# Ninety-six-slot expert units in a two-block network kernel, with the overflow blocks looped in threes

## The chip, the core and the metric

The kernel runs on one core of a Trainium2 chip. The metric is device time in microseconds (us), lower is better. A median of three runs is given; one further execution was taken by the hardware profiler and gives every row shown here.

## The reference, cut to what matters

The network has 512 tokens of width 1024. The first block ends in a mixture of experts, and that part is what the change touches:

```
logits = xt @ router_w + router_b                 # 512 tokens x 32 experts
top_val, top_idx = lax.top_k(logits, 4)           # every token goes to 4 experts
gate = softmax(top_val)
gu   = xblk @ w_gu[e] + b_gu[e]                   # 1024 -> 2048: gate half g, up half up
act  = (min(up, 7, -7 clipped) + 1) * (g * sigmoid(1.702 * g)),   g = min(g, 7)
y    = act @ w_down[e] + b_down[e]                # 1024 -> 1024
out[token] += y * gate                            # over the 4 experts of a token
```

So there are 2048 token places over 32 experts, 64 on average. For the inputs as they are drawn, the router of the reference gives expert 0 21 tokens, and the other 31 experts, the fullest first: 173, 125, 102, 101, 94, 94, 93, 89, 86, 85, 80, 80, 76, 72, 66, 64, 61, 60 and so on down to 5. All arithmetic is in 32-bit floats. The second block (attention, a state-space scan, a convolutional feed-forward part) follows and isn't touched.

## The kernel before, in words

**Units.** The experts are worked off in 33 units, in a fixed order that the core knows before it has seen the tokens (`expert_units`, L45 to L53). Expert 0 comes first; the others are ranked by their number of tokens on the core, and a unit belongs to a rank. A large unit has 128 slots (expert 0 and the ranks 0 to 14), a small one has 64 (the ranks 15 to 30, and one more for the tokens 128 to 191 of rank 0). Large and small units alternate: even unit numbers are large, odd ones small, the last (32) is small. A token that finds no slot goes to an extra block of 128 slots after the units; `dve_extra_lists` (L1646) makes the list of them, 16 long, from the capacities in `RANK_CAPS` (L58).

**A unit on TensorE (PE).** Weights come as panels of 1024 x 512 (2 MB each): two for the gate half, two for the up half, two for down. The tokens' features are the stationary operand and the weight panel is the moving one. In a large unit (`pe_expert_in`, L1773; `pe_expert_out`, L1805) each panel takes 8 matmuls of 128 slots x 512 columns, one after the other. In a small unit the 64 slots are put in twice: the lower 64 columns of the array work on the first panel while the upper 64 work on the second, so that one pass of 8 steps covers both panels, and the result has slots of the first half of the columns in partitions 0 to 63 and of the second half in 64 to 127. Here a "beat" is one 32-bit pass of 512 moving columns; a matmul in 32-bit floats is two records in the profile and takes two beats.

**The order on PE** (`pe_moe`, L1858): gate(u), down(u-1), up(u), then the next u. Smaller work is put in between the steps (`between`): the transposes of the activations of u-1 in gate(u); in up(u) the matmuls that make the slot list of u+2 (`pe_slots`, L1488, 4 matmuls against the 0/1 matrix `sel`), the transposes of the gathered tokens of u+1, and the shares of u-1. A **share** (`pe_share`, L1840) sends the result of an expert back to the tokens: per 128 features a one-pass matmul of a high and a low part against `tokens_r`, four visits of two feature tiles each. A share of a small unit uses the array in two row halves that work at once, and waits until both of its PSUM banks are free (L1850).

**The other engines.** VectorE (DVE) clips the gate and up results, multiplies, and adds each share to `hidden` (L1946), which frees the bank for the next share. ScalarE (ACT) copies transposes and scales results. GpSimd (POOL) gathers the tokens of unit u by an indirect DMA and lays out the expert columns for the bias. SyncE (SP) loads the weight panels in order into six slots; each load waits until PE has given the slot back (`Panels.load`, L172).

**The extra blocks.** `extra_blocks` (L2005) is a loop of 16 turns on each of PE, ACT, DVE and SP. Each turn reads the block's number from memory and branches over the body when it is zero. DVE moves the common counter `turn` on for a skipped block, and ACT and SP wait for 16 blocks' worth of it before the next stage (L2107, L3350, L2204); PE has to leave its own loop.

Of the kernel before, what the change touches and what calls it, by code (L numbers as in the profile page):

```python
# [14 lines left out]
P = 128  # L15
# [28 lines left out]

def expert_units():  # L45
# [12 lines left out]
RANK_CAPS = [(NE, S), (NE - 1, HALF - S), (15, S - HALF), (1, HALF)]  # L58
# [168 lines left out]
def constants():  # L227
# [16 lines left out]
    parts["block_start"] = np.broadcast_to(S * np.arange(-1, XBLOCKS)[None, :], (P, XBLOCKS + 1))  # L244
# [30 lines left out]
def build(nc, a, table, where, out):  # L275

    ctx = ExitStack()
    with ctx:
# [25 lines left out]
        with ExitStack() as over:  # L304
# [4 lines left out]
            tokens_r = over.enter_context(nc.sbuf_tensor("tokens_r", [P, T], F32R))  # L309
            perm_r = over.enter_context(nc.sbuf_tensor("expert_of_rank", [P, 2, NE], F32R))  # L310
            both_r = over.enter_context(nc.sbuf_tensor("expert_of_unit", [P, 3, S], F32R))
        IOTA_AT = 8192 + 3 * D + T + 2 * NE + 3 * S
# [987 lines left out]
        router_w = part(IOTA_AT + T, DT, NE)  # L1300
        r_at = [IOTA_AT + T + DT * NE]

# [6 lines left out]
        logits, cur, hot, cand, chosen, expo, im64, posm, posr, perm = (r_part(TT, NE) for _ in range(10))  # L1309
# [5 lines left out]
        cmp_t = r_part(16, NE)  # L1315
        bgu = r_part(NE, 16)
        slot_vals = r_part(N_UNITS, 2)
        slot_tok = r_part(N_UNITS).bitcast(I32)
        unit_expert = r_part(N_UNITS)[0:1, :].bitcast(I32)
        extra_e = sb("extra_expert", [1, 16], I32)  # L1320
        extra_b = sb("extra_block", [1, 16], I32)
# [33 lines left out]
        def chunks(u):  # L1355
            return UNITS[u][2] // HALF
# [8 lines left out]
        def small_no(u):  # L1365
            return sum(chunks(v) == 1 for v in range(u))
# [121 lines left out]
        def pe_slots(pe, mm, banks, u):  # L1488
# [3 lines left out]
            for t in range(TT):  # L1492
                vals = gate_0[:, t, :] if u == 0 else gate_r[:, t, r:NE + 1:NE - r]
                ins = mm(bank[:, 0:2], sel[:, u % 2, t, :], vals, t == 0, t == TT - 1)
                if t == TT - 1:
                    ins.then_inc(banks.full, 1)
# [149 lines left out]
        def dve_extra_lists(dve, step):  # L1646
# [27 lines left out]
            cj = c1.rearrange("p (j e) -> p j e", j=1).broadcast_to([1, 16, NE])  # L1674
            jj = con("iota", 16)[0:1, :].rearrange("p (j e) -> p j e", e=1).broadcast_to([1, 16, NE])
            ct = cmp_t[0:1, :, :]
            xe, xb, xt = x_e[0:1, 0:16], x_b[0:1, 0:16], x_t[0:1, 0:16]
# [4 lines left out]
            tt(ct, ct, n1.rearrange("p (j e) -> p j e", j=1).broadcast_to([1, 16, NE]), ALU.mult).then_inc(dve_done, 1)  # L1682
# [3 lines left out]
            tt(xb, con("iota", 16)[0:1, :], xb, ALU.subtract).then_inc(dve_done, 1)  # L1686
# [25 lines left out]
        def dve_select(dve, u):  # L1712
# [5 lines left out]
            else:  # L1718
                ins = dve.tensor_tensor(sel[:, u % 2, :, :].rearrange("p t (h s) -> p t h s", h=2),
                                        iota_t[:, off:off + HALF].rearrange("p (t h s) -> p t h s", t=1, h=1)  # L1720
                                        .broadcast_to([P, TT, 2, HALF]),
                                        pos.rearrange("p t (h s) -> p t h s", h=1).broadcast_to([P, TT, 2, HALF]),
                                        ALU.is_equal)
            ins.then_inc(sel_ready.sem, 1)

        def dve_slots(dve, banks, u):
            dve.wait_ge(banks.full, banks.next_full())
            bank = banks.take()
            dve.tensor_copy(slot_tok[:, u:u + 1], bank[:, 1:2])
            dve.tensor_copy(slot_vals[:, u, :], bank[:, 0:2]).then_inc(banks.free, 1)  # L1730
# [17 lines left out]
        def act_turn_x(act, u):  # L1748
            for i in range(chunks(u)):
                act.wait_ge(moe_t.full, moe_t.next_full())  # L1750
                bank = moe_t.take()
                act.activation(xg[u % 2][:, i * 512:(i + 1) * 512], bank[:, :], ACT.Copy).then_inc(moe_t.free, 1)
# [3 lines left out]
        def pe_turn_act(pe, mm, u, i):  # L1756
            pe.wait_ge(act_ready.sem, act_ready.next(pe))
            pe.wait_ge(moe_t.free, moe_t.room())
            bank = moe_t.fill()
            for b in range(4):  # L1760
                ins = mm.transpose(bank[:, b * P:(b + 1) * P], ub[:, i * 512 + b * P:i * 512 + (b + 1) * P], ident)
                if b == 3:
                    ins.then_inc(moe_t.full, 1)

        def act_turn_act(act, u):
            for i in range(chunks(u)):
                act.wait_ge(moe_t.full, moe_t.next_full())
                bank = moe_t.take()
                act.activation(moe_act_t[:, i * 512:(i + 1) * 512], bank[:, :], ACT.Copy).then_inc(moe_t.free, 1)  # L1769
# [3 lines left out]
        def pe_expert_in(pe, mm, u, banks, bias, between):  # L1773

            r, off, n = UNITS[u]
            x = xg[u % 2].rearrange("p (k s) -> p k s", s=n) if n == S else \
                xg[u % 2][:, 0:DT * HALF].rearrange("p (k s) -> p k s", s=HALF)
# [19 lines left out]
            for k in range(DT):  # L1797
                for c, (s, w) in enumerate(pair):
                    ins = mm(bank[c * HALF:(c + 1) * HALF, :], x[:, k, :], w[:, k, :], k == 0, False)
                    if k == DT - 1:  # L1800
                        ins.then_inc(panels.used[s], 1)
                between(k)
            mm(bank[:, :], both_r[:, small_no(u) % 3, :], bias, False, True).then_inc(banks.full, 1)

        def pe_expert_out(pe, mm, u):  # L1805
            if chunks(u) == 2:
# [21 lines left out]
            for k in range(DT):  # L1828
                for c, (s, w) in enumerate(pair):
                    ins = mm(moe_y(no)[c * HALF:(c + 1) * HALF, :], t[:, k % 4, k // 4, :], w[:, k, :],  # L1830
                             k == 0, k == DT - 1)
                    if k == DT - 1:
                        ins.then_inc(shares_full if c else panels.used[s], 1)
# [1583 lines left out]
```

## Time and profile before

| | |
|---|---|
| median of 3 runs | 3785.39 us (3784.65 to 3787.49) |
| the profiled execution | 3785.36 us |
| its span | 3783.5 us |
| PE busy | 3310.6 us, 88% |
| DVE busy | 1276.8 us, 34% |
| ACT busy | 496.9 us, 13% |
| loaded from memory | 577.65 MB, 154 GB/s over the span |

The span is the time from the first to the last instruction of the profiled execution; 1.9 us of its own time lie around it. Busy shares are averages over stages with different limits, so the stage that a change touches has to be read by itself. PE's matmuls are pipelined: a record is longer than the distance to the next, and distances between starts are what counts. The clock that PE was granted is 1.00 (2.4 GHz) or 0.50 (1.2 GHz) of full speed.

### The profile page before, as it was taken

What the parts mean: (1) busy time and instruction counts of PE and PEld (TensorE: products, weight loads), DVE (VectorE), ACT (ScalarE), POOL (GpSimd) and SP (SyncE); (2) the same over time, 40 slices, a digit from 0 to 9 for tenths busy, and PEclk for the clock granted to TensorE, in tenths of its full rate; (3) what the DMA queues carried; (4) which work ended last, traced back from release to release, by engine and by line L of the source; (5) the groups of instructions that cost most, each with busy time, mean ns of one, the idle gap of its engine ahead of it and who ended that gap; (6) DMA issues with size and microseconds to landing.
All of it is one profiled execution on the core that took longest, in us unless ns stands there. A gap on an engine that the chain in (4) does not pass through costs nothing.

```text
span 3783.5 us, 28754 instructions
## 1 busy us (share of the span) xinstructions
PE 3310.6 (88%) x11091; PEld 1625.8 (43%) x11092; DVE 1276.8 (34%) x2053; ACT 496.9 (13%) x853; POOL 252.1 (7%) x279
## 2 busy tenths in 40 slices
PE   4894758799999999999994797887868999899998
PEld 2352223544444444444441555535636444344444
DVE  2127982422322323223233338804334110222101
ACT  1211002200000010000100211112214100100000
POOL 0005540100000000000000001200000000000000
PEclk8986779699999999999997797897779999999999
DMA  9412411389899898998984010011010122212210
GB/s 291 167 67 75 145 45 31 128 320 339 312 340 339 321 341 311 340 339 321 341 313 166 23 45 12 1 39 34 1 45 1 56 78 73 72 67 78 71 63 22
DMA packets 288045, 583.67 MB, mean 154 GB/s; under 512 B 7953, under 2 KB 12492, under 8 KB 287884
## 3 DMA queue, kind: packets, MB, share of 16 engines
q1 hardware_dynamic: 281184, 561.20, 41.3%
q0 software_dynamic: 5456, 17.38, 1.9%
q10 hardware_dynamic: 1276, 3.29, 0.2%
q8 instruction: 91, 1.49, 0.2%
q14 instruction: 38, 0.31, 0.0%
HBM read 577.65 MB, written 4.19 MB: 154 GB/s over the span
## 4 chain that ended last, share of the span: by engine, by line
PE 77%; DVE 14%; ACT 3%; issue 2%; SPq 1%; POOL 1%; ACTq 1%; DMA 1%; DVEq 0%; POOLq 0%; PEldq 0%
PE psum_all L206 74%; DVE scratch L1190 4%; PE psum_all L214 3%; SPq L183 1%; DVE scratch L1214 1%; DVE scratch L2562 1%; DVE scratch L2975 1%; ACTq L559 1%; DVE scratch L2593 1%; DVE scratch L1207 1%; ACT scratch L3037 1%; DVE scratch L2590 1%; DMA panel<-in_ada_w 1%; DVE scratch L2856 0%; ACT hidden L417 0%
## 5 line engine op out<-in xcount | busy, mean ns | idle before, releaser
L206 PE MATMUL psum_all<-panel,scratch 128*64 128x512 f32 (+3 forms) x3264 | 1100.5, 595 | 1.6 <-ACTq L1771 0.8
L206 PE MATMUL psum_all<-hidden,panel 128*128 128x512 f32 (+1 forms) x1808 | 794.0, 601 | 31.2 <-ACT hidden L417 20.9
L206 PEld LDWEIGHTS psum_all<-panel,scratch 128*128 128x128 f32 (+1 forms) x3264 | 400.9, 165 | 523.0 <-issue 517.7
L206 PEld LDWEIGHTS psum_all<-hidden,panel 128*128 128x128 f32 (+1 forms) x1808 | 346.3, 192 | 470.1 <-issue 439.7
L206 PE MATMUL psum_all<-scratch 128*128 128x64 f32 (+7 forms) x1592 | 392.7, 443 | 147.1 <-DVEq L1228 82.4
L206 PEld LDWEIGHTS psum_all<-scratch 128*128 128x128 f32 (+1 forms) x1592 | 252.2, 241 | 256.6 <-issue 98.4
L1946 DVE TENSOR_TENSOR hidden<-hidden,psum_all 128x512 f32<-128x512 f32 x264 | 169.6, 684 | 282.7 <-PE psum_all L206 282.7
L214 PE MATMUL psum_all<-const,scratch 128*128 128x128 f32 (+3 forms) x977 | 156.4, 300 | 112.3 <-DMA scratch<-in_s_lambda_im 33.4
L206 PE MATMUL psum_all<-scratch,panel 128*128 128x512 f32 (+1 forms) x672 | 250.5, 531 | 2.0 <-DVE resid L3162 1.0
L214 PEld LDWEIGHTS psum_all<-const,scratch 128*128 128x128 f32 (+3 forms) x977 | 115.3, 156 | 208.8 <-issue 102.1
L206 PE MATMUL psum_all<-scratch,const 128*128 128x512 f32 (+4 forms) x212 | 107.7, 664 | 95.4 <-ACT scratch L408 44.8
L206 PEld LDWEIGHTS psum_all<-scratch,panel 128*128 128x128 f32 x672 | 127.5, 190 | 127.5 <-issue 119.6
L1936 DVE SCALAR_TENSOR_TENSOR y_low<-psum_all,scratch,y_high 128x512 fp32r<-128x512 f32 x49 | 36.8, 750 | 312.8 <-ACT y_high L1910 312.8
L206 PE MATMUL psum_all<-panel,hidden 128*128 128x512 f32 (+2 forms) x384 | 113.2, 460 | 10.4 <-ACT hidden L417 10.4
L1927 DVE TENSOR_SCALAR scratch<-psum_all 128x512 f32<-128x512 f32 x49 | 33.9, 691 | 261.4 <-PE psum_all L206 261.4
L206 PE MATMUL psum_all<-panel 128*128 128x512 f32 x256 | 110.5, 593 | 1.7 <-DVEq L3153 1.7
L1404 POOL DMA_INDIRECT scratch<-token_rows,scratch x33 | 31.3, 948 | 1195.3 <-DVEq L1732 1195.3
L1769 ACT ACTIVATE scratch<-psum_all 128x512 f32<-128x512 f32 x49 | 29.3, 597 | 620.5 <-PE psum_all L214 620.5
L206 PEld LDWEIGHTS psum_all<-scratch,const 128*128 128x128 f32 (+1 forms) x212 | 46.9, 250 | 148.0 <-issue 81.5
L1190 DVE TENSOR_TENSOR scratch<-scratch 128x512 f32<-128x512 f32 x128 | 104.8, 840 | 4.6
L2451 DVE TENSOR_SCALAR scratch<-psum_all,cols 128x512 f32<-128x512 f32 (+1 forms) x44 | 33.0, 750 | 193.2 <-PE psum_all L206 193.2
L206 PE MATMUL psum_all<-tokens_r,y_high 64*128 64x512 f32 (+1 forms) x264 | 91.9, 477 | 6.8 <-DVE hidden L1946 5.2
(309 smaller groups left out, 2313.6 us busy)
## 6 DMA issues: line engine op xcount, KB each, us to landing
panel<-in_exp_w_gu SPq DMA_DIRECT2D x132, 2048.0 KB, 10.7
panel<-in_exp_w_down SPq DMA_DIRECT2D x66, 2048.0 KB, 10.8
panel<-in_w_in SPq DMA_DIRECT2D x17, 2048.0 KB, 8.2
panel<-in_ada_w SPq DMA_DIRECT2D x12, 2048.0 KB, 20.3
panel<-in_w_mod SPq DMA_DIRECT2D x12, 2048.0 KB, 7.8
panel<-in_ffn_w_gate SPq DMA_DIRECT2D x5, 2048.0 KB, 7.8
panel<-in_ffn_w_up SPq DMA_DIRECT2D x5, 2048.0 KB, 7.8
panel<-in_w_out SPq DMA_DIRECT2D x4, 2048.0 KB, 8.0
```

The costliest lines, as they stand in the source:

```text
L183: sp.dma_start(dst, src.rearrange("(k p) c -> p k c", p=P)).then_inc(self.loaded[s], 16)
L206: ins = self.pe.matmul(out, lhsT, rhs, start=start, stop=stop)
L214: return self.pe.transpose(out, in_, ident)
L559: act.dma_start(rows[at:at + n, tile_no, :], flat(name).rearrange("(r c) -> r c", c=P))\
L1190: tt = lambda o, x, y, op: dve.tensor_tensor(o, x, y, op)
L1207: dve.tensor_tensor_scan(z_re, mag, w1, 0.0, ALU.mult, ALU.add).then_inc(dve_done, 1)
L1214: dve.tensor_tensor_scan(z_im, mag, w3, 0.0, ALU.mult, ALU.add).then_inc(dve_done, 1)
L1946: dve.tensor_tensor(hidden[:, m, :], hidden[:, m, :], moe_y(no)[:, :], ALU.add).then_inc(shares_free, 1)
L2562: tt = lambda o, x, y, op: dve.tensor_tensor(o, x, y, op)
L2590: dve.tensor_tensor(decay[g][:, 4 * i:4 * i + 4, :], over(head_cols(acs, d, c, g)[:, 4 * i:4 * i + 4], P), bank[:, :].rearrange("p (h i) - ...
L2593: dve.tensor_scalar(decay[g], decay[g], 0.0, None, ALU.max).then_inc(dve_done, 1)
L2975: dve.tensor_reduce(tmp_max[:, 0:1], pair[:, 512 - w:768], AX_X, ALU.max).then_inc(dve_done, 1)
```

## The change

The units of expert 0 and of the ranks 4 to 14, twelve in all, get 96 slots in place of 128. Expert 0 and the ranks' capacities change with them. A unit of 96 is computed as 64 slots in the two halves of the array, as a small unit is, and then 32 slots in four strips of 32 columns, each strip with 256 columns of a panel (strips 0 and 1 on the first panel, 2 and 3 on the second). Both panels are needed at its start and given back at its end. Its selection matrix is made twice (`sel` and `sel_last`), its slot list takes 8 matmuls, its shares take 8 matmuls a visit in place of 4 (four in row halves, four in row quarters), and its `tokens_r` is made twice. POOL lays out four more pieces for the bias. The list of extra blocks is 21 long, and the loops go over it in seven groups of three: a group is skipped as a whole when its first block is empty, and otherwise all three bodies run. SP's separate early load for the first extra block is gone.

```diff
-    large = [(NE - 1, 0, S), (0, 0, S)] + [(r, 0, S) for r in range(1, 15)]
+    large = [(NE - 1, 0, 96), (0, 0, S)] + [(r, 0, S if r < 4 else 96) for r in range(1, 15)]
...
-RANK_CAPS = [(NE, S), (NE - 1, HALF - S), (15, S - HALF), (1, HALF)]
+CHUNKS = {S: (512, 512), 96: (512, 256), HALF: (512,)}
+RANK_CAPS = [(NE, 96), (NE - 1, -32), (15, 32), (4, 32), (1, 64)]
...
@@ pool_moe @@
                 if u == 0:
                     pool.wait_ge(perm_ready.sem, perm_ready.next(pool))
-                if n == HALF:
-                    both = both_r[:, small_no(u) % 3, :]
+                    pool.memset(quarter_r[:, :, :, :].bitcast(F32), 0.0).then_inc(pool_done, 1)
+                    pool.wait_ge(pool_done, step.next())
+                if n < S:
+                    both = both_r[:, halved_no(u) % 4, :]
...
+                    if n == 96:
+                        for q in range(4):
+                            pool.tensor_copy(quarter_r[:, quartered_no(u) % 2, q % 2, q * QUARTER:(q + 1) * QUARTER],
+                                             perm_r[:, q // 2, r:r + 1].broadcast_to([P, QUARTER])).then_inc(pool_done, 1)
+                        pool.wait_ge(pool_done, step.next(4))
@@ pe_slots @@
-            for t in range(TT):
-                vals = gate_0[:, t, :] if u == 0 else gate_r[:, t, r:NE + 1:NE - r]
-                ins = mm(bank[:, 0:2], sel[:, u % 2, t, :], vals, t == 0, t == TT - 1)
+            sels = [sel[:, u % 2, :, :], sel_last][:2 if UNITS[u][2] == 96 else 1]
+            for i, slots_at in enumerate(sels):
+                for t in range(TT):
+                    vals = gate_0[:, t, :] if u == 0 else gate_r[:, t, r:NE + 1:NE - r]
+                    ins = mm(bank[:, 2 * i:2 * i + 2], slots_at[:, t, :], vals, t == 0, t == TT - 1)
@@ pe_expert_in @@
             for k in range(DT):
                 for c, (s, w) in enumerate(pair):
-                    ins = mm(bank[c * HALF:(c + 1) * HALF, :], x[:, k, :], w[:, k, :], k == 0, False)
+                    ins = mm(bank[c * HALF:(c + 1) * HALF, :], x[:, k, 0:HALF], w[:, k, :], k == 0, False)
...
+                if n == HALF:
+                    between(k)
+                elif k % 2:
+                    between(k // 2)
+            mm(bank[:, :], both_r[:, halved_no(u) % 4, :], bias, False, True).then_inc(banks.full, 1)
+            if n == HALF:
+                return
+            pe.wait_ge(banks.free, banks.room())
+            bank = banks.fill()
+            for k in range(DT):
+                for q in range(4):
+                    s, w = pair[q // 2]
+                    ins = mm(bank[q * QUARTER:(q + 1) * QUARTER, 0:256], x[:, k, HALF:96],
+                             w[:, k, q % 2 * 256:q % 2 * 256 + 256], k == 0, False)
+                    if k == DT - 1 and q % 2:
+                        ins.then_inc(panels.used[s], 1)
+                if k % 2:
+                    between(4 + k // 2)
+            for i in range(2):
+                ins = mm(bank[:, 0:256], quarter_r[:, quartered_no(u) % 2, i, :], bias[:, i * 256:(i + 1) * 256], False, i == 1)
+            ins.then_inc(banks.full, 1)
@@ pe_expert_out: after the halves @@
+            if n == 96:
+                t = moe_act_t[:, 512:768].rearrange("p (b q s) -> p b q s", b=2, q=4)
+                no = y_fill(u, 1)
+                pe.wait_ge(shares_free, no)
+                pe.wait_ge(act_turned.sem, act_turned.next(pe))
+                for k in range(DT):
+                    for q in range(4):
+                        s, w = pair[q // 2]
+                        ins = mm(moe_y(no)[q * QUARTER:(q + 1) * QUARTER, 0:256], t[:, k % 2, k // 2, :],
+                                 w[:, k, q % 2 * 256:q % 2 * 256 + 256], k == 0, k == DT - 1)
...
@@ pe_share, a unit under 128: after the high and low parts of the halves @@
+            f = slice(512 + m % 2 * P, 512 + (m % 2 + 1) * P)
+            quarters = [slice(q * QUARTER, (q + 1) * QUARTER) for q in (m // 2, m // 2 + 2)]
+            for h, no in zip(quarters, nos):
+                mm(moe_y(no)[:, :], y_hi[h, f], tokens_r[h, 1, :], False, False)
+            for h, no in zip(quarters, nos):
+                mm(moe_y(no)[:, :], y_lo[h, f], tokens_r[h, 1, :], False, True).then_inc(shares_full, 1)
@@ dve_select @@
+                copies = [(sel[:, u % 2, :, :], off, HALF)]
+                if n == 96:
+                    copies.append((sel_last, off + HALF, QUARTER))
@@ extra_blocks @@
-            with eng.Fori(first, 16) as j:
-                block_no = eng.value_load(extra_b[0:1, bass.ds(j, 1)], min_val=0, max_val=XBLOCKS)
+            with eng.Fori(0, EXTRAS // GROUP) as group:
+                block_no = eng.value_load(extra_b[0:1, bass.ds(group * GROUP, 1)], min_val=0, max_val=XBLOCKS)
                 with eng.If(block_no > 0):
-                    e = eng.value_load(extra_e[0:1, bass.ds(j, 1)], min_val=0, max_val=NE - 1)
-                    taken(j, e, block_no)
+                    for i in range(GROUP):
+                        j = group * GROUP + i
+                        b = eng.value_load(extra_b[0:1, bass.ds(j, 1)], min_val=0, max_val=XBLOCKS) if i else block_no
+                        e = eng.value_load(extra_e[0:1, bass.ds(j, 1)], min_val=0, max_val=NE - 1)
+                        taken(j, e, b)
```

## Rows read from the trace of the kernel before

**Rows 1.** The page: the span, PE's share, its granted clock in 40 slices.
```profile
span 3783.5 us, 28754 instructions
...
PE 3310.6 (88%) x11091; PEld 1625.8 (43%) x11092; DVE 1276.8 (34%) x2053; ACT 496.9 (13%) x853; POOL 252.1 (7%) x279
...
PEclk8986779699999999999997797897779999999999
```

**Rows 2.** Busy us by stretch: PE, PEld, DVE, ACT, POOL; then PEclk, DMA share, GB/s.
```profile
1121.76:1200.45 78.69, 78.69 (x276) 32.97 (x275) 23.27 (x39) 7.54 (x12) 2.29 (x4) 1.00 0.92 330
...
1098.68:1102.62 3.94, 3.94 (x19) 1.55 (x17) 0.97 (x3) 0.69 (x1) 0.18 (x1) 1.00 1.05 388
1110.49:1114.42 3.93, 3.93 (x16) 1.50 (x15) 2.55 (x4) 0.00 (x0) 0.00 (x0) 1.00 0.02 4
```

**Rows 3.** Timeline of weight loads: 128 columns; 64, in pairs; 32, in fours.
```profile
1123.26 0.19 PEld L206 LDWEIGHTS psum_all<-panel,scratch 128*128 128x128 f32 x1 [0.24 <-issue]
...
1157.51 0.14 PEld L206 LDWEIGHTS psum_all<-panel,scratch 128*64 128x64 f32 x2 [0.29 <-issue]
...
46.73 0.13 PEld L206 LDWEIGHTS psum_all<-panel,silus 128*32 128x32 f32 x4 [0.30 <-issue]
```

**Rows 4.** Timeline of PE in one large and one small unit.
```profile
1129.59 9.00 PE L206 MATMUL psum_all<-panel,scratch 128*64 128x512 f32 x36
1138.42 0.95 PE L206 MATMUL psum_all<-scratch,slots_of_units 128*128 128x2 f32 x8
1139.23 1.96 PE L206 MATMUL psum_all<-panel,scratch 128*128 128x512 f32 x4
...
1148.20 0.50 PE L206 MATMUL psum_all<-tokens_r,y_high 64*128 64x512 f32 x2
...
1148.87 1.98 PE L206 MATMUL psum_all<-panel,scratch 128*128 128x512 f32 x4
...
1156.17 3.65 PE L206 MATMUL psum_all<-panel,scratch 128*64 128x512 f32 x16
1159.76 0.66 PE L214 MATMUL psum_all<-const,scratch 128*128 128x128 f32 x4
...
1164.65 14.90 PE L206 MATMUL psum_all<-panel,scratch 128*128 128x512 f32 x36
...
1184.67 0.50 PE L206 MATMUL psum_all<-tokens_r,y_high 128*128 128x512 f32 x1
...
1185.80 1.08 PE L206 MATMUL psum_all<-panel,scratch 128*64 128x512 f32 x4
1186.80 0.50 PE L206 MATMUL psum_all<-tokens_r,y_high 128*128 128x512 f32 x1
...
1193.20 0.50 PE L206 MATMUL psum_all<-bias_rows,expert_of_unit 128*128 128x512 f32 x1
1193.54 7.03 PE L206 MATMUL psum_all<-panel,scratch 128*128 128x512 f32 x16
```

**Rows 5.** Timeline after the last unit, where nothing lies between two shares.
```profile
2020.85 0.50 PE L206 MATMUL psum_all<-tokens_r,y_high 64*128 64x512 f32 x2 [1.58 <-DVE y_low L1936]
...
2021.61 1.29 DVE L1946 TENSOR_TENSOR hidden<-hidden,psum_all 128x512 f32<-128x512 f32 x2 [0.82 <-PE psum_all L206]
2022.95 0.50 PE L206 MATMUL psum_all<-tokens_r,y_high 64*128 64x512 f32 x2 [1.38 <-DVE hidden L1946]
```

**Rows 6.** Branches of the extra blocks' loop (ns min/median/max, first to last us).
```profile
L2009 DVEq COMPARE_BRANCH  x16: 56/56/72, 2031.6 to 2052.1; - x16
L2009 PEldq COMPARE_BRANCH  x16: 208/208/3807, 2031.6 to 2056.4; - x16
```

**Rows 7.** Timeline: the first matmul after that loop; a selection; small transposes.
```profile
2056.96 5.41 PE L206 MATMUL psum_all<-scratch,const 128*128 128x512 f32 x6 [28.09 <-ACT scratch L408]
...
704.56 0.69 DVE L1717 TENSOR_TENSOR slots_of_units<-const,scratch 128x512 f32<-128x512 f32 x1
...
692.04 1.18 PE L214 MATMUL psum_all<-const,scratch 32*128 32x32 f32 x16
```

More of the change, by code:

```diff
@@ L1299, in build @@
         iota_t = part(IOTA_AT, T)
-        router_w = part(IOTA_AT + T, DT, NE)
-        r_at = [IOTA_AT + T + DT * NE]
+        router_w = part(ROUTE_AT, DT, NE)
+        logits, cur, hot, expo, im64 = (part(ROUTE_AT + DT * NE + i * P, TT, NE) for i in range(5))
+        r_at = [IOTA_AT + T]
         def r_part(*shape):
@@ L1308, in build @@
         router_b = r_part(NE)
-        logits, cur, hot, cand, chosen, expo, im64, posm, posr, perm = (r_part(TT, NE) for _ in range(10))
+        cand, chosen, posm, posr, perm = (r_part(TT, NE) for _ in range(5))
         row_max, row_min, top, total = (r_part(TT) for _ in range(4))
@@ L1363, in moe_y, with halved_no, quartered_no @@
             return psum[4 + (no - 1) % 2]
-        def small_no(u):
-            return sum(chunks(v) == 1 for v in range(u))
+        def halved_no(u):
+            return sum(UNITS[v][2] < S for v in range(u))
+        def quartered_no(u):
+            return sum(UNITS[v][2] == 96 for v in range(u))
+        sel_last = con("chunk_keep").rearrange("p (t s) -> p t s", s=S)
         def pool_moe_loads(pool):
@@ L1756, in pe_turn_act @@
         def pe_turn_act(pe, mm, u, i):
+            cols = chunk_cols(u, i)
+            n = (cols.stop - cols.start) // P
             pe.wait_ge(act_ready.sem, act_ready.next(pe))
@@ L1759, in pe_turn_act @@
             bank = moe_t.fill()
-            for b in range(4):
+            for b in range(n):
                 ins = mm.transpose(bank[:, b * P:(b + 1) * P], ub[:, i * 512 + b * P:i * 512 + (b + 1) * P], ident)
-                if b == 3:
+                if b == n - 1:
                     ins.then_inc(moe_t.full, 1)
@@ L1766, in act_turn_act @@
             for i in range(chunks(u)):
+                cols = chunk_cols(u, i)
                 act.wait_ge(moe_t.full, moe_t.next_full())
                 bank = moe_t.take()
-                act.activation(moe_act_t[:, i * 512:(i + 1) * 512], bank[:, :], ACT.Copy).then_inc(moe_t.free, 1)
+                act.activation(moe_act_t[:, cols], bank[:, 0:cols.stop - cols.start], ACT.Copy).then_inc(moe_t.free, 1)
                 act.wait_ge(moe_t.free, moe_t.own_reads())
@@ L2028, in sp_extra @@
             sp.wait_ge(extras_ready.sem, extras_ready.next(sp))
-            block_no = sp.value_load(extra_b[0:1, 0:1], min_val=0, max_val=XBLOCKS)
-            with sp.If(block_no > 0):
-                e = sp.value_load(extra_e[0:1, 0:1], min_val=0, max_val=NE - 1)
-                for i in range(6):
-                    if i < 4:
-                        sp.wait_ge(panels.used[X_PANELS[i]], panels.loads[X_PANELS[i]].value())
-                    else:
-                        sp.wait_ge(turn, stage(0, 4))
-                    load(e, i).then_inc(extra_w, 16)
-            with sp.Else():
-                sp.sem_inc(extra_w, LOADS)
-            sp.end_ifs()
             sp.wait_ge(moe_done.sem, moe_done.next(sp, 3))
@@ L2052, in skipped @@
                 sp.wait_ge(turn, stage(j, 0))
-                sp.sem_inc(extra_w, LOADS)
-            extra_blocks(sp, taken, skipped, first=1)
+                sp.sem_inc(extra_w, GROUP * LOADS)
+            extra_blocks(sp, taken, skipped)
         def dve_extra(dve, step):
```

143 lines of the change are left out of this document (86 added, 57 removed).

## The prediction

> **What bounds the kernel now.** Start with the page [rows 1]: PE is busy 88% of the span, and its clock stands at full speed from about a third of the span to a little past half, which is the expert stage. Cut that stage into stretches of one large and one small unit (from 807 to 1987 us there are fifteen, all 78.69 us): PE is busy for all of each, DVE for 23.27 us, ACT for 7.54 [rows 2]. Loading isn't the limit there. In the same 78.69 us the core moves 330 GB/s, 25.97 MB, while a stretch in which it is kept supplied moves 388 GB/s, and there are gaps with almost nothing (4 GB/s), when all six slots are full [rows 2]. At 388 GB/s a pair of units would need 66.9 us. So a pair is 78.69 us of PE's stream, and 11.8 us can go before the loads take over.
>
> The timeline [rows 4] cuts that stream. A beat (one pass of 512 columns) is 0.43 us: a weight load and the idle time behind it, 0.19 + 0.24 [rows 3]. Two loads of 64 columns come in the same 0.14 + 0.29, so the two halves of the array really work at once. The pair is: gate of the large unit 14.74 us (its start is 1193.54 - 78.69 = 1114.85, to 1129.59), down of the small one 7.12 (to 1138.42, less the four full-width records, 1.72), up of the large one 19.46 (to 1156.17), gate of the small one 8.48 (to 1164.65), down of the large one 13.73 (32 beats), up of the small one 15.16 (to 1193.54). Smaller prices: slot list of 4 matmuls 0.81 (1138.42 to 1139.23), a share of a small unit 0.67 (1148.20 to 1148.87), of a large one 1.13 (1184.67 to 1185.80), four transposes about 0.58 (0.66 long), a bias 0.34 (1193.20 to 1193.54). Two beats between shares take 1.00 rather than 0.86 (1185.80 to 1186.80), so going from one division of the array to another costs 0.07.
>
> After the units every engine runs the loop over 16 empty extra blocks. DVE's branches go from 2031.6 to 2052.1, 1.37 us a turn; PE's from 2031.6 to 2056.4, of which the first took 3.81 and the others come every 1.38 [rows 6]. The next matmul starts at 2056.96 [rows 7], half a microsecond after PE's last branch. The trace names ACT as its releaser; PE's own loop was later.
>
> **Does the data still fit?** With the counts in the section on the reference, expert 0 has 21 tokens for 96 slots, ranks 4 to 14 have 94 to 66 for 96, rank 15 has 64 for 64. Nothing overflows, all seven groups are skipped.
>
> **The strips.** The one thing not in today's expert stage is four strips of 32 columns. The modulation stage has them with 512 moving columns: four weight loads in 0.13 + 0.30 us [rows 3], four matmuls a beat. With 256 columns I take half a beat, 0.215, for four. The lower bound is that. The upper bound is four weight loads that can't be hidden: then a strip part takes what the eight steps of the halves take, 16 beats, 6.86 us, in place of 3.44. I take the low end since the row with strips is the nearest: the loads need 0.13 us, less than 0.215.
>
> **A unit of 96, phase by phase** (each division change 0.07).
> - Gate: 16 beats 6.86, four transposes 0.58, bias 0.34, strips 16 x 0.215 = 3.44, two short biases 0.34, changes 0.3: 11.9, against 14.74.
> - Down of the small unit before: 7.0 (one change fewer).
> - Up: 6.86 + 3.44, slot list of the next 96-unit 2 x 0.81 = 1.62, transposes 0.64, four shares 2.68, biases 0.68, fourteen changes 0.98: 16.9. Here a wait appears. Where nothing lies between, shares follow each other in 2.10 us (2020.85 to 2022.95): the matmuls, DVE's two additions of 1.29, the way there and back [rows 5]. In the strips there is only 4 x 0.215 of work between shares, 1.67 us with the share. So PE waits 0.43 twice, a little before the first: 1.0. Up is 17.9, against 19.46. The wait stands in PE's queue, so the next steps and all of gate(u+1) are behind it.
> - Gate of the next small unit: two transposes fewer, 8.3.
> - Down: 6.86 + 3.44 + 0.2 = 10.5, against 13.73.
> - Up of the small unit: its four shares now have 8 matmuls, 0.67 more each. They wait for both banks: 2.10 + 0.67 = 2.77 from one to the next, against 1.13 + 1.00 = 2.13. Three distances give +1.9, the last share +0.2: 17.3, against 15.16.
>
> Sum 72.9, against 78.69: **5.8 us less for each of the 11 pairs** of ranks 4 to 14, 63.8. Unit 0 has no shares of its own to wait for: gate -2.8, up -3.0, down -3.2, transposes -0.2, the shares in unit 1 +2.1: 7.1 less. Together 70.9.
>
> Loads: a pair keeps its 12 panels, its gather shrinks by 32 rows; at 66.9 us it stays below 72.9. Two panels come free at once and not one by one, so loads come in bursts, but three pairs of slots, 11 us of loading each, cover phases of 7 to 18 us. I cost this at nothing; its cover is 6 us a pair. SP's queue isn't changed within the units.
>
> Added on DVE and POOL: a second selection (0.69) [rows 7] and a second token matrix for each 96-unit, on a DVE that is busy 30% of a pair; four pieces on a POOL that is busy 3% [rows 2]. Unit 0's second selection stands in the chain to the first gather: +0.7. The longer lists run beside gate(0).
>
> The loop: nine turns fewer, PE's 9 x 1.38 = **12.4 less**; DVE's and ACT's, which start the norm, shrink alike. SP's early load was skipped anyway.
>
> Total -70.9 - 12.4 + 0.7 = -82.6, from the profiled execution's 3785.36 (span 3783.5), which is the median of the runs within 0.03 us: **3703 us**.
>
> **A rule that speaks against it.** The trace has the next four strip weight loads under the running matmuls [rows 3]. The Trainium skill, TensorE: Matmul & The Clock Gate, Part 3, states that a weight load overlaps running matmuls only when its row group differs; column strips share the row group. By it the strips would lose their gain, the case of 3826 below. The row disagrees with it. The same section gives 2.38 times for three column strips, 79% of the ideal; by that figure the strips would take 4.35 us and not 3.44, and the total would be 3736.
>
> **Rivals.**
> - **Strips no faster than halves.** Weight loads, or the two records that each matmul puts on one strip in turn, hold the four strips apart. Each strip part costs 6.86: +3.42 x 3 parts x 12 units = +123, 3826 us, slower. It decides from 5.7 us a part on (3.44 plus 82.6 / 36). For it: no row has strips with 256 columns. Against: the four-fold rows.
> - **PE can't be fed fast enough.** The densest run of single matmuls is 16 in 1.18 us, 0.074 each [rows 7]. Strips want 0.054. At 0.074 a part takes 4.74: +1.3 x 36 = +47, 3750.
> - **The branch over three bodies.** PE's first branch took 3.81 us, the others 0.208 [rows 6]: its code had to be fetched once. A body is now three times as long. If head and end of the loop no longer stay at hand together, 13 more branches cost 3.6: +47, 3750. The Trainium skill, Runtime: NRT & Kernel Launch, Instruction fetch mechanics, gives PE room for 2048 instructions, fetches a branch target outside a window of two pages, and says so of every taken branch. With about 750 instructions to a body, three don't fit. The later branches of 0.208 over more than two pages speak against the strict form.
> - **The additions aren't late.** DVE and PE interleave as today: up loses only its work and no wait, and a pair saves about 7.7: 3680.
> - **Loads in twos.** If pairs of panels released together keep the pair near 78.7 us after all, the 11 pairs give nothing: 3767. Against: 66.9.
> - **It doesn't do what it says.** A rank over its capacity runs a group of three blocks, 18 panels of 5.4 us, about 100 us more: slower. The counts exclude it, by two tokens at rank 4.
>
> **How the numbers follow.** Forecast 0.57; additions not late 0.12; feeding 0.08; branches 0.09; loads 0.06; strips 0.07; overflow 0.01. The range leaves out the last three and some of the edges: 3677 to 3753. The forecast alone, with changes of division at half or twice their price and waits off by a third, is 3688 to 3722. About 0.2% is what the measurement can tell from no change. Faster: all but strips and overflow, 0.92; within 0.2%: 0.01; slower: 0.07.
>
> **What would show it.** Pairs from rank 4 on at 73 us, the first four at 78.7. Weight loads of 32 columns in fours every 0.215 us. Shares of 96-units 2.8 us apart, with PE idle before them and DVE's addition as releaser. DVE's branches x7, PE's x7 with one long, and the first norm matmul about 17 us after the last share. It is wrong if strip loads come in fours every 0.43, if PE waits for panels, or if a norm starts late behind several long branches.

## The result, and the profile after

The changed kernel takes 3698.89 us (median of 4 runs, 3698.03 to 3700.76), the kernel before 3785.19 beside it (3784.65 to 3787.49). The ratio is 0.9773, 95% interval 0.9759 to 0.9788: 86 us less. The forecast was 3703. The profiled execution has a span of 3697.6 us against 3783.5.

The page, as for before in [rows 1]: the span, PE's share, its granted clock.

```profile
span 3697.6 us, 33767 instructions
...
PE 3222.1 (87%) x13683; PEld 1566.0 (42%) x13684; DVE 1277.0 (35%) x2091; ACT 486.5 (13%) x853; POOL 264.7 (7%) x352
...
PEclk8896769699999999999996897896879999999999
```

PE has 2592 more matmul records and is busy 88 us less: the strips are passes of 256 columns and not 512, and four of them run at once. DVE has the same load as before, although it got 38 instructions more.

Busy time of one pair of units, columns as in [rows 2]: a 96 and a 64 from rank 4 on, then one of the first four pairs, which the change leaves alone.

```profile
1251.56:1324.55 72.99, 71.15 (x492) 28.10 (x492) 23.20 (x42) 6.69 (x12) 3.35 (x10) 1.00 0.99 355
957.65:1036.34 78.69, 78.69 (x276) 32.96 (x275) 23.89 (x40) 7.54 (x12) 2.29 (x4) 1.00 0.92 330
```

The pairs from rank 4 on are 5.70 us shorter each. The first pairs stay at 78.69. PE is no longer busy all of a pair: 1.84 us are gaps. The core now moves 355 GB/s instead of 330, since the same panels are loaded in less time.

The timeline of PE through one unit of 96 and a small one, which answers to [rows 4]:

```profile
1254.32 7.09 PE L211 MATMUL psum_all<-panel,scratch 128*64 128x512 f32 x32
...
1262.16 3.66 PE L211 MATMUL psum_all<-panel,scratch 128*32 128x256 f32 x64
...
1266.19 8.80 PE L211 MATMUL psum_all<-panel,scratch 128*64 128x512 f32 x40
1274.92 1.05 PE L211 MATMUL psum_all<-scratch,slots_of_units 128*128 128x2 f32 x8
...
1283.98 1.07 PE L211 MATMUL psum_all<-panel,scratch 128*32 128x256 f32 x16
1284.99 0.50 PE L211 MATMUL psum_all<-tokens_r,y_high 64*128 64x512 f32 x2
...
1285.66 1.07 PE L211 MATMUL psum_all<-panel,scratch 128*32 128x256 f32 x16
1287.10 0.49 PE L211 MATMUL psum_all<-tokens_r,y_high 64*128 64x512 f32 x2 [0.37 <-DVE hidden L2039]
...
1291.30 3.65 PE L211 MATMUL psum_all<-panel,scratch 128*64 128x512 f32 x16
...
1299.65 11.69 PE L211 MATMUL psum_all<-panel,scratch 128*64 128x512 f32 x100
...
1316.24 0.50 PE L211 MATMUL psum_all<-tokens_r,y_high 64*128 64x512 f32 x2
...
1319.01 0.50 PE L211 MATMUL psum_all<-tokens_r,y_high 64*128 64x512 f32 x2 [0.37 <-DVE hidden L2039]
...
1321.78 0.50 PE L211 MATMUL psum_all<-tokens_r,y_high 64*128 64x512 f32 x2 [0.36 <-DVE hidden L2039]
...
1324.55 0.50 PE L211 MATMUL psum_all<-tokens_r,y_high 64*128 64x512 f32 x2 [0.37 <-DVE hidden L2039]
...
1327.31 7.09 PE L211 MATMUL psum_all<-panel,scratch 128*64 128x512 f32 x32
```

A strip part is 64 records in 3.59 us (1262.16 to 1265.75). Five shares of a pair now have PE idle ahead of them, released by DVE's addition into hidden (the bracket behind a row: idle time, and what ended it). Where a share has no such wait, it follows 1.01 us after the strips began; with it, 1.44 us (1285.66 to 1287.10). So each wait costs 0.43, though the bracket shows 0.37.

The weight loads of those strips (timeline of PEld), the loop's branches as in [rows 6], and the first norm matmul as in [rows 7]:

```profile
1283.98 0.59 PEld L211 LDWEIGHTS psum_all<-panel,scratch 128*32 128x32 f32 x16 [0.25 <-issue]
```

```profile
L2102 PEldq COMPARE_BRANCH  x7: 208/215/3837, 1962.4 to 1974.7; - x7
L2102 DVEq COMPARE_BRANCH  x7: 56/56/72, 1962.4 to 1971.9; - x7
```

```profile
1975.31 2.90 PE L211 MATMUL psum_all<-scratch,const 128*128 128x512 f32 x3 [15.61 <-ACT scratch L415]
```

Sixteen strip loads take 0.59 us and lie inside the 1.07 us of their matmuls: they don't add to them. The first branch of PE takes 3.84 us and the other six about 0.21, with a body three times as long.

### The profile page after: what moved, and what is told of

It is laid out like the page before. It is cut to its first block, busy times and chain, and to the rows that moved or that the text cites. A ratio compares the mean times of both kernels' runs of the same rounds, so it can differ in the third digit from the quotient of the medians.

```text
span 3697.6 us, 33767 instructions
## 1 busy us (share of the span) xinstructions
PE 3222.1 (87%) x13683; PEld 1566.0 (42%) x13684; DVE 1277.0 (35%) x2091; ACT 486.5 (13%) x853; POOL 264.7 (7%) x352
## 4 chain that ended last, share of the span: by engine, by line
PE 75%; DVE 16%; ACT 3%; issue 2%; SPq 1%; POOL 1%; ACTq 1%; DMA 1%; DVEq 0%; POOLq 0%; PEldq 0%
PE psum_all L211 72%; DVE scratch L1197 4%; PE psum_all L219 3%; DVE hidden L2039 2%; SPq L188 1%; DVE scratch L1221 1%; DVE scratch L2646 1%; DVE scratch L3059 1%; DVE scratch L2677 1%; ACTq L566 1%; DVE scratch L1214 1%; ACT scratch L3121 1%; DMA panel<-in_ada_w 1%; DVE scratch L2674 1%; DVE scratch L2940 1%
## 5 line engine op out<-in xcount | busy, mean ns | idle before, releaser
L211 PE MATMUL psum_all<-panel,scratch 128*64 128x512 f32 (+3 forms) x5568 | 977.7, 507 | 1.4 <-ACTq L1814 0.8
L211 PEld LDWEIGHTS psum_all<-panel,scratch 128*64 128x64 f32 (+2 forms) x5568 | 333.8, 131 | 472.7 <-issue 426.1
L219 PE MATMUL psum_all<-const,scratch 128*128 128x128 f32 (+4 forms) x953 | 150.6, 297 | 111.5 <-DMA scratch<-in_s_lambda_im 33.0
L219 PEld LDWEIGHTS psum_all<-const,scratch 128*128 128x128 f32 (+4 forms) x953 | 109.7, 155 | 211.4 <-issue 105.2
L211 PE MATMUL psum_all<-scratch,const 128*128 128x512 f32 (+5 forms) x308 | 120.2, 535 | 82.8 <-ACT scratch L415 32.3
L2029 DVE SCALAR_TENSOR_TENSOR y_low<-psum_all,scratch,y_high 128x512 fp32r<-128x512 f32 (+1 forms) x49 | 33.6, 686 | 271.5 <-ACT y_high L2001 271.5
L211 PE MATMUL psum_all<-tokens_r,y_high 64*128 64x512 f32 (+2 forms) x360 | 97.0, 496 | 28.2 <-DVE hidden L2039 26.6
L211 PEld LDWEIGHTS psum_all<-scratch,const 128*128 128x128 f32 x308 | 59.1, 235 | 135.0 <-issue 68.2
L1812 ACT ACTIVATE scratch<-psum_all 128x512 f32<-128x512 f32 (+1 forms) x49 | 26.7, 545 | 617.8 <-PE psum_all L219 617.8
L2019 DVE TENSOR_SCALAR scratch<-psum_all 128x512 f32<-128x512 f32 (+1 forms) x49 | 30.7, 626 | 218.6 <-PE psum_all L211 218.6
```

Of the source, the lines that this page charges most:

```text
L211: ins = self.pe.matmul(out, lhsT, rhs, start=start, stop=stop)
L219: return self.pe.transpose(out, in_, ident)
```

## The experiments

Spans and points in time below are those of each run's one profiled execution. e4, e6, e7, e8, e9 and e10 have one run each, so for them the stretches of the trace are compared and not the totals. A "loop time" is the distance from the end of DVE's last addition to the norm's first matmul: 26.77 us before, 14.29 after.

**e1_loop_only: the new loop with the old units.**

```
 # kernel before
+EXTRAS, GROUP = 21, 3      # and extra_blocks, the lists and SP's loop as in the diff
 large = [(NE - 1, 0, S), (0, 0, S)] + [(r, 0, S) for r in range(1, 15)]
```

> The old units (all large ones 128 slots) with the new loop: seven turns over groups of three blocks in place of sixteen over single ones, and the longer lists of 21. My theory: nine turns less at 1.38 us each on PE, the norm starts 12.4 us earlier, nothing before it moves: 3773 us. Rival, a branch over three bodies must fetch its target at every turn: each turn of PE costs 3.8 instead of 1.38, 7 x 3.8 = 26.6 against 24.5 before, so 3785 or more. Rival, the longer lists on DVE delay the units: the last addition comes later than in the kernel before by the delay, and the gain is smaller than 12.4. Either way a sum check: what this kernel gains and what the units alone gain should add to the 86 us of the full change.

Measured: 3767.46 us, ratio 0.9954 (0.9937 to 0.9970). The loop time is 13.89 us, 12.88 less than before. The units stand as they did: every pair 78.69. The total is 5.5 us better than expected, and hardly because of the loop. In the profiled execution, 15.1 us shorter than before, the stage ahead of the first unit ended 1.9 us later, and behind the loop 4.1 us were gained, 3.1 of them at one place that is looked at below. The rivals of a dear branch and of late lists fall: the 1.9 us are already there 38 us before the first gate, and the units themselves take as long as before.

**e2_units_only: groups of one block, 21 turns.**

```
-EXTRAS, GROUP = 21, 3
+EXTRAS, GROUP = 21, 1
```

> The changed kernel with groups of one block: 21 turns instead of 7, the units of 96 kept. My theory: 14 turns more at 1.38 us, +19.3 on the 3698.9 of the changed kernel: 3718 us, and the units before the loop end at the same time. From the kernel before: 70 us from the units, less 5 turns more (6.9), and the 3 us that the full change gained far downstream if they belong to the units. Rival, the turn of a group costs more than the turn of a single block (longer bodies): then the difference is below 19.3, down to 14 x 1.38 - 7 x the surplus.

Measured: 3720.99 us, ratio 0.9836 (0.9819 to 0.9852), 22 over the changed kernel. The loop time is 33.76, that is 19.47 more than with seven turns, 1.39 a turn. Pairs are 72.98. A turn over three bodies costs the same as a turn over one. The units, from the first gate to the last addition, take 1231.26 us in both kernels.

**e3_groups_of_7: three turns, bodies seven times as long.**

```
-EXTRAS, GROUP = 21, 3
+EXTRAS, GROUP = 21, 7
```

> The changed kernel with three groups of seven blocks, bodies seven times as long. My theory: PE's first branch takes its 3.8 us whatever the length, four turns less at 1.38: -5.5, 3693.4 us. Rival, the fetch depends on how far the branch goes: from seven bodies (some 5000 instructions) each branch costs 3.8 us: 3 x 3.8 + the rest = 3 x 5 = 15 us of loop against 7 x 1.38 + 2.4 = 12.1: 3702 us.

Measured: 3695.29 us (3691.36 to 3700.32), ratio 0.9768 (0.9752 to 0.9785). The loop time is 8.63, 5.66 less than with seven turns. The branches of this kernel, columns as above:

```profile
L2102 DVEq COMPARE_BRANCH  x3: 56/56/72, 1958.8 to 1964.8; - x3
L2102 PEldq COMPARE_BRANCH  x3: 215/221/3880, 1958.8 to 1965.4; - x3
```

One branch of 3.88, the others 0.22: the long one doesn't grow with the body and doesn't come again. With 3, 7, 12, 16, 19 and 21 turns the loop times are 8.63, 14.29, 21.07, 26.77, 30.98 and 33.76 (12 and 19 from two runs below): some 4.6 us and 1.38 a turn. The median moved by 3.6 us only, with runs 9 us apart. In the span it is 7.0: the stage ahead of the first unit ended 3.6 us sooner than in the changed kernel, and 2.3 were lost behind the loop, where the granted clock differs (the last experiment).

**e4_two_strips_of_four: half of the strips left out.** Strips 1 and 3 aren't computed in the six middle steps of each strip part.

```
-                for q in range(4):
+                for q in range(4) if k in (0, DT - 1) else (0, 2):     # in and out
```

> The changed kernel, but in the six middle steps of each strip part only strips 0 and 2 are computed (half of the columns of the last 32 slots is left out there). Theory, the four strips run side by side and a step of k takes 256 columns whatever the number of strips, 0.43 us for both records of each: nothing changes, a pair stays at 73.0 us. Rival, the strips are bound by how fast matmuls or weight loads can be issued (0.054 us each): six steps take half, 3 parts x 6 x 0.215 = 3.9 us less a pair, 69.1, and 43 us less in all. Rival in between, pairs of strips share something: less than 3.9 us but not 0.

Measured: 3695.93 us in one run, a pair 72.96 against 72.99. Two pieces of a unit's up, timeline of PE in this kernel:

```profile
1283.89 1.06 PE L211 MATMUL psum_all<-panel,scratch 128*32 128x256 f32 x12
1284.89 0.50 PE L211 MATMUL psum_all<-tokens_r,y_high 64*128 64x512 f32 x2
...
1285.55 1.06 PE L211 MATMUL psum_all<-panel,scratch 128*32 128x256 f32 x8
```

Eight records take the 1.06 us that sixteen took (1.07 in the changed kernel). So a strip part is bound by the 256 columns that pass, and the third and fourth strip are free. This excludes a limit by issue or by weight loads at this density. (The total is 3 us lower: half of it is the last unit's down, 8.45 us here and 10.05 in the changed kernel. That unit has no strips, so it isn't what the edit did; at full clock the same 32 records take 7.09.)

**e5_spread_shares: the same work, the shares further apart.**

```
-                    if i in (3, 4, 5, 6) and u:
-                        pe_share(pe, mm, u - 1, 2 * (i - 3))
+                    if u and i in share_at(u):
+                        pe_share(pe, mm, u - 1, 2 * share_at(u).index(i))
+            # share_at: (1, 3, 5, 7) in a unit of 64 after one of 96,
+            #           (2, 3, 5, 7) in a unit of 96, else (3, 4, 5, 6)
```

> The changed kernel with only the places of the shares moved: in a small unit after one of 96 they stand behind steps 1, 3, 5, 7 and not 3 to 6; in a unit of 96 behind 2, 3, 5, 7. Theory, PE waits for DVE's additions because the shares stand too close: the five waits of 0.37 us in a pair go, DVE keeps its work and its slack of 0.5 us before the next transposes: a pair takes 71.1 in place of 73.0, 11 pairs give 20 us: about 3678 us. Rival, the waits only move (DVE's last addition now ends later and its activation step delays the transposes in the next gate): the last wait of 0.37 comes back as 0.5 to 1 us before the transposes and the gain is 9 us or less. Rival, loads: a faster pair meets the load floor: with 66.9 us as the floor nothing is seen, with a floor over 71.1 the pair stays above it.

Measured: 3666.76 us (3665.63 to 3669.73), ratio 0.9690 (0.9674 to 0.9706): another 32 us. A pair in this kernel (windows, then the timeline of PE in it):

```profile
1203.04:1273.40 70.36, 70.36 (x493) 28.40 (x492) 23.09 (x42) 6.69 (x12) 3.36 (x10) 1.00 1.02 368
```

```profile
1203.04 0.49 PE L211 MATMUL psum_all<-tokens_r,y_high 64*128 64x512 f32 x2
...
1205.57 0.50 PE L211 MATMUL psum_all<-tokens_r,y_high 64*128 64x512 f32 x2
...
1206.67 1.93 PE L211 MATMUL psum_all<-panel,scratch 128*32 128x256 f32 x32
1208.53 0.51 PE L211 MATMUL psum_all<-tokens_r,y_high 64*128 64x512 f32 x2
...
1209.19 1.93 PE L211 MATMUL psum_all<-panel,scratch 128*32 128x256 f32 x32
1211.06 0.50 PE L211 MATMUL psum_all<-tokens_r,y_high 64*128 64x512 f32 x2
```

No bracket is left in the pair, and PE is busy for all of it. It was the additions, and the waits didn't come back elsewhere. The gain is larger than expected, 2.62 us a pair against 1.85: five waits of 0.43 are 2.15. The rest fits the price of cutting the steps into stretches: 16 strip records take 1.01 us from start to next start (1283.98 to 1284.99 above), 32 take 1.86 (1206.67 to 1208.53), so each stretch adds 0.16 to its matmuls, and the new order has three fewer, 0.48. This last part is worked out, not measured by itself; e8 looks at it.

**e6_load_floor: less work for PE, the same loads.** Units of 96 leave out six of eight steps of each strip part and two of eight of each halves part.

```
-                for q in range(4):
+                for q in range(4 if k in (0, DT - 1) else 0):
-                for c, (s, w) in enumerate(pair):
+                for c, (s, w) in enumerate(pair if n == HALF or k not in (3, 4) else []):
```

> The changed kernel with all its loads, but units of 96 leave out six of eight steps of each strip part and two of eight steps of each halves part: 3 x (6 x 0.43 + 2 x 0.86) = 12.9 us less PE work in a pair, 60.1 us, which is below the load floor that the prediction worked out, 25.97 MB at 388 GB/s = 66.9 us. My theory: a pair now takes 66.9 us and PE waits for panels. Rival, loads in twos: the panels come free in bursts and the core moves less than 388 GB/s, so that a pair takes 70 us or more. Rival, the loads can go faster than 388 GB/s: a pair nearer to 60.

Measured: 3640.87 us in one run. Nine pairs together, PE's waits in the same stretch, and the widest single pair of this kernel:

```profile
1191.74:1807.14 615.40, 558.89 (x2892) 207.64 (x2892) 207.92 (x376) 60.17 (x108) 29.52 (x86) 0.93 1.04 377
```

```profile
PE psum_all L211 <- DVE hidden L2039: 38.0, 54, 1.4
PE psum_all L211 <- issue: 18.4, 12, 2.9
```

```profile
1530.19:1605.21 75.02, 67.06 (x324) 25.47 (x324) 23.20 (x42) 6.69 (x12) 3.35 (x10) 0.86 1.05 378
```

68.4 us a pair on average, 377 GB/s, against the 66.9 expected at 388. Single pairs go from 65.1 to 75.0. But only a third of PE's waits can be for panels: 38.0 us of them, 54 waits, six in a pair, end with DVE's addition, since fewer steps now lie between two shares. The other 18.4 us, 12 waits, have no releaser in the trace and stand before panel matmuls. Beside the waits the granted clock is 0.93 on average and 0.86 in the widest pair, so PE's own work takes longer too (62.1 us busy a pair where 60.1 was expected). What speaks for the loads as a limit is the DMA share, 1.04 over nine pairs, where the stretch at 388 GB/s in [rows 2] has 1.05. So 68.4 is what a pair takes with all of this together and not a floor of the loads alone, and e5's 70.4, at a share of 1.02, is close to it. How much of the last 2 us the loads would allow isn't shown.

**e8_spread_full_units: the spread where nothing waits.**

```
+                if n == HALF and prev == S:
+                    return 1, 3, 5, 7
+                return (3, 4, 5, 7) if n == S else (3, 4, 5, 6)
```

> The changed kernel with the shares moved only where nothing waits for DVE: in small units after one of 128 behind steps 1, 3, 5, 7, in units of 128 behind 3, 4, 5, 7. It separates the two terms of the spread shares' gain (2.62 us a pair, where five waits account for 5 x 0.43 = 2.15). Theory, the rest is the price of a change between divisions of the array: each stretch of steps between two other things costs 0.15 us more than its matmuls (a stretch of four matmuls takes 1.01, not 0.86), and three fewer stretches give 0.45. Then a pair of 128 and 64 slots gets two stretches fewer in the small unit and one in the large: 78.69 - 0.45 = 78.24. Rival, it all came from the waits: 78.69 stays.

Measured: 3695.8 us in one run; the pairs of 128 and 64 take 77.98 against 78.69, 0.71 less where 0.45 was expected. There were no waits to remove, so an order with fewer stretches does gain. But all of it comes from the small unit, where two stretches went (both kernels run the large one in the same time), so one is worth 0.36 between shares of the full array. The 0.16 is not a general price; what makes the difference wasn't separated.

**b1_spread_groups_of_7: both together.** The shares spread in all units, and three groups of seven.

```
+                return {HALF: (1, 3, 5, 7), 96: (2, 3, 5, 7), S: (3, 4, 5, 7)}[n]
-EXTRAS, GROUP = 21, 3
+EXTRAS, GROUP = 21, 7
```

> The version that should beat both: shares spread in all units (1, 3, 5, 7 in small ones, 2, 3, 5, 7 in those of 96, 3, 4, 5, 7 in those of 128) and three groups of seven blocks. From what was measured: 3666.8 for the shares spread beside units of 96, less 4 x 1.38 = 5.5 for the groups, less 4 x 0.45 = 1.8 for the first four pairs: 3659.5 us. Rival, the faster pairs of 70.4 us come near the load floor (68.4 us a pair on average where PE did less) and now and then wait for a panel: up to 10 us more. Rival, the gains at the ends of units don't add: 3665.

Measured: 3658.12 us (5 runs, 3654.0 to 3664.97), ratio to the kernel before 0.9665 (0.9652 to 0.9678). It beats both kernels: 126 us below the one before, 41 below the changed one. Its five runs are 11 us apart, and the profiled one is the longest of them. Pairs take 77.98 and 70.37, PE never waits in them, and the loop time is 8.85. Seven blocks in a group have a price that no run here shows: an input in which one expert overflows would compute seven blocks for it, not three.

**e7_before_again, e9_before_4_turns_less, e10_before_3_turns_more: where 3 us come from that nobody worked for.** Between 2915 and 2940 us (time of before) the changed kernel gains 3.1 us in a stage of the same code, and so does e1. First the kernel before once more; then its units with another count of turns.

```
 # kernel before with the rewritten loop
-EXTRAS, GROUP = 21, 3
+EXTRAS, GROUP = 12, 1      # e9
+EXTRAS, GROUP = 19, 1      # e10
```

> The kernel before, unchanged, profiled once more. In every kernel profiled so far but that one a stretch of its second half, some 850 us before the end, takes 3.1 us less, and the granted clock there is higher; the kernel with only the new loop shows it too. Theory, chance: a second profile of the same kernel can have the short form, about 3780 us in all, or the long one. Rival, it hangs on where the expert stage ends: then the second profile shows the 3.1 us again, since nothing has moved. The start of the kernel (before the first unit) differed by up to 6 us between kernels that have the same code there: theory, it differs here as well.

> The kernel before with its units, and a loop of 12 single blocks instead of 16: what follows the loop runs about 4 x 1.38 = 5.5 us earlier and is the same code. In the kernel before (profiled twice) the granted clock fell to half for 6.5 us at 2922 us; in each kernel whose end came 12 us or more sooner it didn't, and 3.1 us were saved. Theory, the dip hangs on when that stage runs, in steps finer than 12 us: with 5.5 us the dip may stand or be gone, and a total shift of 5.5 or of 8.6 us says which. Rival, the dip belongs to the kernel's state before the loop, or to the form of the loop over groups: then 5.5 and the dip stands in both kernels of this call.

> The kernel before with a loop of 19 single blocks: what follows runs about 3 x 1.38 = 4.1 us later. Theory, the dip hangs on when the stage runs: a shift of -4.1 with the dip, or of about -1 without it. Rival, any later start keeps the dip: -4.1.

The totals are 3786.89 (e7), 3778.66 (e9) and 3783.3 us (e10). The spans are 1.6 us longer than before's, 6.7 shorter and 2.0 shorter, so e9 and e10 moved by none of the sizes that were expected. In e7 the first gate stands at 731.96 us, in before at 730.49: as expected, the stage ahead of the units differs between two profiles of one kernel too.

One group of twenty matmuls at that place, timeline of PE; first the kernel before, then e7, the changed kernel, and b1:

```profile
2915.07 2.94 PE L206 MATMUL psum_all<-scratch 128*128 128x64 f32 x20
...
2923.47 5.52 PE L206 MATMUL psum_all<-scratch 128*128 128x64 f32 x20
```

```profile
2925.05 5.52 PE L206 MATMUL psum_all<-scratch 128*128 128x64 f32 x20
```

```profile
2840.09 2.94 PE L211 MATMUL psum_all<-scratch 128*128 128x64 f32 x20
```

```profile
2802.97 5.52 PE L211 MATMUL psum_all<-scratch 128*128 128x64 f32 x20
```

The same matmuls, at 2.4 or at 1.2 GHz: in before the granted clock over 2920 to 2931 us is 0.69, while in e1, over the same code 12 us sooner, it is 1.00. The group accounts for 2.6 of the 3.1 us, ten transposes just ahead of it for the rest. The second profile of before has the slow group again, which makes chance unlikely. e9 and e10 have it too (5.52 us at 2916.85 and 2921.42), the changed kernel, e1 to e6 and e8 don't, b1 does. So it hangs neither on the loop's form (e2 and e9 both loop over single blocks) nor on the units (e1 has those of before and isn't slow, b1 has those of 96 and is) nor simply on coming earlier (b1 comes 120 us earlier). That the moment at which the stage runs decides is what is left, but it is argued: the granted clock of the stages just before it differs between these kernels as well. e9 and e10 show more of this between 2500 and 2730 us: e9 ran 10.0 us ahead of before at the start of that stretch and 6.7 at its end; e10 ran 1.4 behind and then 2.0 ahead, though its loop was 4.2 longer. What runs behind a moved stage can thus give or take some 3 us with no edit to it. What sets the moments stays open.

## Why the prediction held, and where two errors cancelled

- **A pair**: forecast 72.9, measured 72.99. By phase, from the timeline: gate of the 96 11.87 (1254.32 to 1266.19; forecast 11.9); down of the small one 7.0 (1266.19 to 1274.92, less 1.72 for two steps of the up; forecast 7.0); up of the 96 18.1 (to 1291.30; forecast 17.9); gate of the small one 8.35 (to 1299.65; forecast 8.3); down of the 96 and up of the small one together 27.66 (to 1327.31; forecast 27.8).
- **The strips**: 64 records in 3.59 us against the 3.44 that was forecast; the low end of the bound was right, and e4 shows why: the columns decide. The rule weighed against them (the Trainium skill, TensorE: Matmul & The Clock Gate, Part 3: a load overlaps running matmuls only when its row group differs) doesn't hold for column strips here, 16 loads lie within 1.07 us of matmuls. By its 2.38 times for three strips a part would have taken 4.35 us (an estimate); the measured 3.59 is 3.8 of four.
- **The additions late**: five waits of 0.43 in a pair. In the up of the 96 they are 0.86, where 1.0 was forecast (the little before the first didn't come); in that of the small one 1.3, as the forecast distance of 2.77 has it. e5 took them away. The rival of 3680, additions not late, falls. The kernel before had the same wait three times in its last unit, at the same distance of 2.11 us from share to share, a nearer row than the one that the forecast used:

```profile
1999.44 0.50 PE L206 MATMUL psum_all<-tokens_r,y_high 64*128 64x512 f32 x2 [0.36 <-DVE hidden L1946]
...
2001.55 0.50 PE L206 MATMUL psum_all<-tokens_r,y_high 64*128 64x512 f32 x2 [0.36 <-DVE hidden L1946]
```

- **Loads**: they didn't bind at 73 us, as forecast. The floor was put at 66.9; with PE's waits for DVE in it e6 came to 68.4, so the floor itself stays unmeasured.
- **The loop**: forecast 12.4, measured 12.48, and 12.88 alone (in e1 PE's first branch took 3.45 us and not 3.81). The price of 1.38 a turn holds from 3 to 21 turns. The branch over three bodies costs nothing more; nor over seven. This speaks against a fetch at every taken branch whose target lies outside two pages (the Trainium skill, Runtime: NRT & Kernel Launch, Instruction fetch mechanics): PE's later branches take 0.21 to 0.22 us at every length tried.
- **Unit 0 and the ends**: here the sum was too good. The units as a whole, from the first gate to the last addition, gave 68.45 us and not 70.9: 62.7 from eleven pairs where 63.8 was worked out, 6.6 from unit 0 where 7.1 stood, and 0.8 lost in the last unit, whose down ran in 10.05 us against 9.25 before, both with the granted clock below full (32 such records take 7.09 at full clock).
- **The second selection of unit 0**: priced at +0.7. The first gate came 0.73 earlier instead, of which 0.67 is a shift that was there before the MoE stage; the selection itself was paid for by smaller transposes.
- **Nothing was forecast behind the norm**, and 4.3 us came from there: 3.1 from the clock at one place. 68.45 + 0.73 + 12.48 + 4.30 = 85.96, the difference of the spans. Against the forecast of 82.6 the units gave 2.4 us less, the start 1.4 more and the part behind the norm 4.3 more: 3.3 in all. So that 3703 came within 4 us of 3699 is in part luck, two errors with opposite signs; the pair and the loop, which carry the change, were right by themselves.

e1 and e2 together say that the parts add: 15.1 and 66.7 us of span, and 7.0 for the five turns that e2 has more than before, are 88.8. Both contain the 3.1, and their starts differ from before's by 1.9 us later and 2.0 earlier; with the 3.1 counted once, that is 85.6 of the 86.

## What to carry to other kernels

In this kernel four strips of a narrow unit cost the columns that pass, so four strips of 256 replace one pass of 512 by half of one; but look at what follows them, since a faster stretch puts the next producer-consumer distance (here two additions of 1.28 us on DVE) in its way. Five waits of 0.43 us in a pair look small, but moving calls to other steps and nothing else gained 29 us in eleven pairs: 24 from the waits, and the rest, it seems, from fewer stretches. Price a loop that mostly skips by its turns.

## What the hardware showed that was not expected

- The same group of twenty matmuls took 2.94 us in the profiles of eight kernels and 5.52 in those of before, e9, e10 and b1, and 5.52 again in a second profile of before; before's total contains 3.1 us of that.
- The stage ahead of the first unit ended between 1.9 us later and 4.3 us earlier than in before (e1, e3), though no edit there was meant to move it; between the two profiles of before it is 1.5.
- PE's first branch over the loop's body costs 3.3 to 4.1 us once (e6, b1), whether it passes one block, three or seven; the 3.3 and 3.8 are both of bodies of three.
- At 377 GB/s and a PE that waits now and then, the granted clock over nine pairs is 0.93 (e6), while in the pairs shown of before, the changed kernel and e5 it is 1.00.
